# The four groups' roots of the first mixer: by transposes on TensorE, or by GpSimd's queue through a scratch tensor

## What is computed

```python
    y = y.reshape(Bsz, S, D_INNER) * jax.nn.silu(z.astype(jnp.float32))
    y = y.reshape(Bsz, S, SSM_GROUPS, D_INNER // SSM_GROUPS)
    y = y * lax.rsqrt(jnp.mean(y * y, axis=-1, keepdims=True) + EPS)
    y = y.reshape(Bsz, S, D_INNER) * g_out.astype(jnp.float32)
    return y.astype(h.dtype) @ w_out
```

## Time and profile before

| what | value |
|---|---|
| median of 3 runs | 1812.09 us (1811.99 to 1812.32) |
| the profiled execution's own time | 1812.19 us |
| its span | 1810.1 us |
| TensorE busy | 1798.2 us, 99% of the span |
| VectorE, ScalarE, GpSimd busy | 57%, 41%, 4% |
| mean granted clock of TensorE | 0.998 |
| DMA, mean over the span | 94 GB/s |

### The profile page before, as it was taken

The page is one execution under the profiler, slowest core; times in us unless marked ns, Lnnn a source line. Parts: engine busy times, 40 slices in busy tenths (PEclk is TensorE's granted clock), DMA queues, the critical chain, the costliest instruction groups (busy, mean ns, idle before and its releaser), DMA issues.

```text
span 1810.1 us, 21187 instructions
## 1 busy us (share of the span) xinstructions
PE 1798.2 (99%) x8374; PEld 1456.9 (80%) x8374; DVE 1039.4 (57%) x1502; ACT 735.6 (41%) x1202; POOL 71.3 (4%) x137
## 2 busy tenths in 40 slices
PE   9999999999999999999999999999999999999998
PEld 7777777888766788888888888888888888888887
DVE  8899986566687565444333356564444544444333
ACT  5788885433477532223222332223222322322221
POOL 1002021001210000000000000000000000000000
PEclk9999999999999999999999999999999999999999
DMA  5477662322211223233333322333333233323331
GB/s 180 92 106 113 111 106 84 98 94 93 70 36 36 82 81 105 93 95 101 96 97 102 117 82 93 96 99 98 94 102 97 94 94 104 93 94 95 103 97 56
DMA packets 50577, 170.84 MB, mean 94 GB/s; under 512 B 5808, under 2 KB 8368, under 8 KB 50480
## 3 DMA queue, kind: packets, MB, share of 16 engines
q1 hardware_dynamic: 47376, 161.44, 28.5%
q0 software_dynamic: 2240, 7.34, 4.9%
q10 hardware_dynamic: 864, 0.72, 0.1%
HBM read 167.31 MB, written 2.16 MB: 94 GB/s over the span
## 4 chain that ended last, share of the span: by engine, by line
PE 94%; DVE 4%; ACT 1%; issue 1%; DMA 0%; DVEq 0%; SPq 0%; ACTq 0%
PE pb L771 28%; PE pb L773 28%; PE pb L772 28%; PE pb L882 2%; PE pb L997 2%; PE pb L1026 1%; PE pb L1002 1%; PE pb L1170 1%; PE pb L1172 1%; PE pb L1171 1%; PE pb L785 1%; DVE wl L1576 0%; DVE CV L1748 0%; PE pb L1180 0%; ACT wr L1228 0%
## 5 line engine op out<-in xcount | busy, mean ns | idle before, releaser
L771 PE MATMUL pb<-XR,wr 128*128 128x512 f32 x1584 | 625.4, 395 | 0.7 <-DVE wl L1576 0.5
L773 PE MATMUL pb<-XR,wl 128*128 128x512 f32 x1584 | 617.0, 390 | 0.0
L772 PE MATMUL pb<-XL,wr 128*128 128x512 f32 x1584 | 616.9, 389 | 0.0
L1576 DVE TENSOR_TENSOR wl<-raw,wr 128x1024 fp32r<-128x1024 f32 (+1 forms) x297 | 358.2, 1206 | 350.7 <-ACT wr L1228 349.6
L1228 ACT ACTIVATE wr<-raw 128x1024 fp32r<-128x1024 f32 (+1 forms) x295 | 305.4, 1035 | 299.3 <-PE pb L773 273.7
L771 PEld LDWEIGHTS pb<-XR,wr 128*128 128x128 f32 x1584 | 297.4, 188 | 65.7 <-issue 3.9
L773 PEld LDWEIGHTS pb<-XR,wl 128*128 128x128 f32 x1584 | 297.4, 188 | 63.0
L772 PEld LDWEIGHTS pb<-XL,wr 128*128 128x128 f32 x1584 | 297.5, 188 | 60.0 <-issue 0.2
L771 PE MATMUL pb<-ffn2HR,wr 128*128 128x512 f32 (+1 forms) x198 | 72.7, 367 | 0.0
L772 PE MATMUL pb<-ffn2HL,wr 128*128 128x512 f32 (+1 forms) x198 | 72.3, 365 | 0.0
L773 PE MATMUL pb<-ffn2HR,wl 128*128 128x512 f32 (+1 forms) x198 | 72.3, 365 | 0.0
(11 more groups left out here) (358 smaller groups left out, 2314.9 us busy)
## 6 DMA issues: line engine op xcount, KB each, us to landing
raw<-in_ffn_in SPq DMA_DIRECT2D x88, 512.0 KB, 3.5
raw<-in_mix_in SPq DMA_DIRECT2D x48, 512.0 KB, 3.5
raw<-in_ssm_in SPq DMA_DIRECT2D x40, 512.0 KB, 4.2
raw<-in_ffn_out SPq DMA_DIRECT2D x32, 512.0 KB, 3.5
DB<-cum POOLq DMA_DIRECT2D x28, 256.0 KB, 8.6
raw<-in_ffn_out SPq DMA_DIRECT2D x16, 384.0 KB, 3.1
raw<-in_mla_in SPq DMA_DIRECT2D x11, 512.0 KB, 3.4
raw<-in_ssm_out_a SPq DMA_DIRECT2D x8, 512.0 KB, 3.3
```

The costliest lines, as they stand in the source:

```text
L771: e.matmul(o, r, xr, start=first, stop=False)
L772: e.matmul(o, r, xl, start=False, stop=False)
L773: return e.matmul(o, l, xr, start=False, stop=last)
L1576: e.tensor_tensor(wl[j % NS][:, 0:width(j)], raw[j % NR][:, 0:width(j)], wr[j % NS][:, 0:width(j)].bitcast(F32), ALU.subtract).then_inc(s_ ...
```

## The change

The rows of the four groups no longer go through TensorE. Behind each group's root GpSimd issues two DMAs: `GN` to a new DRAM tensor `grows` (a column of four to four rows, 512 pieces of 4 B), and, when that has landed (`s_gout`), the 2 KB of that group's row to all 128 partitions, into `CH`. The second waits until `CH` is free: for group 0 until the four decays on TensorE are done, for the others until VectorE has scaled the group before. VectorE's scaling waits for that landing (`s_grow`) and reads `CH` in SBUF in the place of a PSUM bank. The wait of the root for the last transposes (`s_spread`) is gone. The scaling of group 3 moves from k-step 5 to k-step 7. The four `spread` calls and their banks are gone, so a few other tiles come to lie in another bank.

```diff
-    tail = {0: [("gfold", 3)], 1: [x[1] for x in due] + [("gsum", 3)], 5: [("gscale", 3)]}
+    tail = {0: [("gfold", 3)], 1: [x[1] for x in due] + [("gsum", 3)], 7: [("gscale", 3)]}
...
+    grows = nc.dram_tensor("grows", (4, 4, 128), F32, kind="Internal").ap()
...
-                elif side == "gscale":
-                    s = f"g{m[0]}"
-                    bk.place("spread " + s, tring.next(), (s_spread, spreads[s] + 1), (s_ynorm, 4 * m[0] + 4))
...
-    bk.place("spread g2", 2, (s_spread, spreads["g2"] + 1), (s_ynorm, 12))
     bk.place("sum g3", 3, (s_sums, sums_no["g3"]), (s_sv, taken["g3"]))
-    bk.place("spread g3", 2, (s_spread, spreads["g3"] + 1), (s_ynorm, 16))
...
-            elif what == "gscale":
-                spread(f"g{m[0]}")
...
             elif what == "gscale":
-                key = f"spread g{m[0]}"
-                w.wait_ge(*bk.full[key])
+                w.wait_ge(s_grow, 16 * m[0] + 16)
                 for t in range(4 * m[0], 4 * m[0] + 4):
                     e.scalar_tensor_tensor(out=YN[:, t, :], in0=YN[:, t, :], scalar=col("g_out", t),
-                                           in1=PB[bk.bank[key]][:, :], op0=ALU.mult, op1=ALU.mult).then_inc(s_ynorm, 1)
+                                           in1=CH[:, :].bitcast(F32), op0=ALU.mult, op1=ALU.mult).then_inc(s_ynorm, 1)
...
             w.wait_ge(s_sv, taken[key])
-            if key in ("g1", "g2", "g3"):
-                w.wait_ge(s_spread, spreads[key])
...
                 e.tensor_tensor(dst[:, :], dst[:, :], GW[:, :], ALU.mult).then_inc(s_groot if i == 2 else c.up(), 1)
+            if key[0] == "g":
+                g = int(key[1])
+                w.wait_ge(s_groot, g + 1)
+                with nc.allow_non_contiguous_dma(reason="a row from a column of four"):
+                    e.dma_start(grows[g].rearrange("i p -> p i"), GN[:, :]).then_inc(s_gout, 16)
+                w.wait_ge(s_gout, 16 * g + 16)
+                if g == 0:
+                    w.wait_ge(s_dec, 4)
+                else:
+                    w.wait_ge(s_ynorm, 4 * g)
+                e.dma_start(CH[:, :].bitcast(F32),
+                            grows[g:g + 1].rearrange("a i p -> a (i p)").to_broadcast([128, S])).then_inc(s_grow, 16)
```

More of the change, by code:

```diff
@@ L459, in build_in @@
     s_groot, s_root, s_spread, s_rs, s_vroot = [sem("s_" + n) for n in ("groot", "root", "spread", "rs", "vroot")]
+    s_gout, s_grow = sem("s_gout"), sem("s_grow")
     s_const, s_warm = sem("s_const"), sem("s_warm")
@@ L506, in build_in @@
     conv_no = {n: i for i, n in enumerate(convs)}
-    spreads = {n: i for i, n in enumerate(("x", "g0", "g1", "g2", "g3", "kv", "ck", "cq", "both", "first", "mix", "f2",
+    spreads = {n: i for i, n in enumerate(("x", "kv", "ck", "cq", "both", "first", "mix", "f2",
                                            "fin0", "fin1"))}
```

## The result

The changed kernel takes **1842.99 us** (median of 4 runs, 1841.56 to 1844.80) against 1812.04 us before (4 runs beside it, 1811.91 to 1812.32): a ratio of 1.0171, 95% interval 1.0159 to 1.0183. It is 31 us slower, where 1811.3 us were forecast, and outside the range. The execution that was profiled is the slowest of the four: it took 1844.80 us, its span is 1843.0 us, and against the profiled execution before (1812.19) it is 32.6 us longer.

The account below looks back on a forecast made before the run. TensorE, busy throughout the stretch, was taken as the bound: -1.76 us for transposes, +0.1 and +0.9 us of waits, -0.8 us from 1812.19 and the median 0.1 lower, so 1811.3 us; range 1810.4 to 1815.7, full range 1810.0 to 1819.5.

Parts of the forecast that it names:

- The 1.76 us: Gain on TensorE from removing four transpose calls, 0.44 us each by the chain that ended last.
- W: Time from issue to landing of the 2 KB write in 512 pieces of 4 B; taken as 4.0 us.
- The rival with 8.6 us: Rows come late: the 512 pieces set the write's time, 8.6 us; +13.0 us, 1825.1 us; chance 0.36 for late by more.
- R: Time from issue to landing of the read, a 2 KB row to 128 partitions; taken as 4.2 us.
- the cover of 7.9 us: Group 0: slack from VectorE's product ending to the heads on TensorE, hiding a decay row 1.1 us late.
- in general W - 1.9: Group 1: how late the decay row of head 28 reaches ScalarE; 2.1 us at the W taken.
- k-steps 4 and 10: Places in ssm_out_a where TensorE would wait for the rows of groups 2 and 3: 0.1 and 0.9 us.
- The formula: Change in kernel time as long as the waits bind: 3W + 2R - 21.2 us.
- I change nothing there: VectorE's scaling of four tiles stays at 2.72 us when the row is in SBUF instead of PSUM.

## Why the prediction was wrong, point by point

- **The 1.76 us.** Not contradicted, and not shown: eight transposes less without any new wait gave 0.92 us (0.88 by the chain's price), but the interval of that ratio holds no change too, and no run has all sixteen gone without another price.
- **W, the step that failed first.** Taken as 4.0 between 1.5 and 8.6, because 256 KB of the decay rows' movement is missing. It is 8.9 to 9.7 us, above the upper end, and neither the bytes nor the number of pieces nor the queue makes it so, but their width of 4 B. The rival with 8.6 us had nearly the right size for a wrong reason: not 512 pieces, since 128 of 4 B took 7.7 to 9.1. R was near: 4.6 to 5.7 for 4.2.
- **A mechanism that no case had.** What is issued while such a write is under way lands only behind it, the decay rows of group 0 by 8.5 to 16.2 us where they were issued beside it. The forecast treated the two transfers as lengths of their own, which others only queue behind. The run that adds only the write lost 7.8 us, as much as a quarter of the loss, with nothing near the write waiting for it.
- **Group 0, the cover of 7.9 us.** The row itself was just in time: it landed at 168.4, and VectorE's scaling began at 168.69, so 0.3 us were to spare where the forecast had 7.7. The decay rows were not, and the cover was misread: "the 7.9 us between the end of VectorE's product" and "the heads on TensorE" leaves out a nearer reader. In the kernel before, ScalarE's gate stands behind the decays, and TensorE's transposes of its tile come at 177.01, ahead of the heads:

```profile
173.33 0.63 ACT L1252 ACTIVATE YN<-CV 128x512 f32<-128x512 f32 x1
```

```profile
177.01 0.60 PE L841 MATMUL pb<-ident,YN 128*128 128x128 f32 x4
```

  173.33 + 0.63 = 173.96, so the cover is 3.05 us. After, that gate stands at 183.39, 10.06 later: 10.06 - 3.05 = 7.0, against the 7.2 us that TensorE waited. The sum also priced only the first of the two decay rows, at 8.6 us; released together, they landed 10.4 and 15.0 us after their issue.
- **Group 1.** The form was right. Its "in general W - 1.9" gives 7.0 us at W = 8.93, and ScalarE waited 7.2; it was carried to group 2's sum as the text says.
- **Groups 2 and 3.** The places were right, k-steps 4 and 10, the sizes not: 5.5 and 7.7 us for 0.1 and 0.9. The formula with the measured means (W = 9.4, R = 5.3) gives 3 x 9.4 + 2 x 5.3 - 21.2 = +17.6, that is 19.4 us of waits beside the gain. The trace has 1.1 + 4.3 + 13.2 = 18.6 outside group 0. What the formula lacked is group 0's 7.2 us and the lower clock behind four of the waits, which the sum put at nothing (8.4 by the rows).
- **VectorE.** "I change nothing there" holds: 2.74 us for four tiles with the row in SBUF, 2.72 in PSUM.
- **The price of a small write.** The fit of the Trainium skill, page "DMA: Bandwidth & Descriptors", section "Anatomy of one DMA — SWDGE (gpsimd) path", gives 2.0 us for the write, an estimate; for 16 B pieces that lies within the 1.7 to 5.3 us measured here, and the traces disagree for 4 B (8.9 to 9.7 in the change). The section "Specifications" of that page of the Trainium skill gives 512 B as the least transfer for full rate; here the cost appeared between 16 B (1.7 to 5.3 us) and 4 B, and pieces of 128 B landed in 2.2 to 3.1 us.

## What to carry to other kernels

Judge a small write to DRAM by the width of its pieces, not by its bytes alone: 4 B against 16 B was 8 to 11 us against 2 to 5 here. Turning a column of scalars so that a partition writes several neighbours at once took 25 us off; who undoes the order has to be priced too, since on both engines tried it made the work longer. When a DMA is added, price what runs beside it and what stands behind it in its queue, every transfer of it, and look for the first reader of the delayed engine's whole queue, not only of the delayed result. A delay costs only where the slack is small: the nine 4 B writes at the end of GpSimd's work made some weight loads beside them land after 8.2 to 12.5 us, and the kernel took no longer (1812.12 us, one run). Where the bounding engine waits, count the lower clock behind the wait beside its length: here 1.4 to 3.0 us for each wait of 4.3 to 7.7.

## What was not expected of the hardware

- A write of 2 KB in 4 B pieces can all but stop the core's DMA for some 7 us: 3 GB/s from 155 to 162 us, 73 without it, and 4 from SP's queue. It does not always: around group 1's write it was 73. Why that is so, and why 4 B differs from 16 B, no run here shows.
- VectorE takes 1.08 us for a tile of 128 x 512 whose second operand is read in steps of four (4.30 for four tiles), 0.68 otherwise; TensorE loads float32 weights in steps of four in 330 ns, 192 otherwise (medians).
- GpSimd's first operation of group 3's root shows 4.64 us in the changed kernel, the next ones 0.20 (group 2's first one: 0.19):

```profile
325.47 4.64 POOL L2318 TENSOR_SCALAR GN<-GV 128x4 int32<-128x4 int32 x1 [7.53 <-DVE GV L1628]
330.19 0.20 POOL L2322 TENSOR_TENSOR GW<-GN 128x4 f32<-128x4 f32 x1
```

  VectorE works there without a gap from 325.30 to 330.05 us. The root took 8.0 us, where the forecast had 6.0. That the one causes the other was not tried, and spans of GpSimd are rough in these profiles.
